# Expert weights in strips of 1024, 1024 and 768 columns over four PSUM banks, hidden rows turned in three groups and the next expert's rows in one

## What is computed

```python
def swiglu(h, w_gu, w_down):
    g, u = jnp.split(h @ w_gu, 2, axis=-1)
    return (jax.nn.silu(g) * u) @ w_down

for e in range(N_EXPERTS):                      # 8 experts, each row goes to 2
    y = y + combine[:, e:e + 1] * swiglu(xf, w_gu[e], w_down[e])
```

## Time and profile before

| what | value |
|---|---|
| median of 3 runs | 1445.33 us (1444.56 to 1445.95) |
| profiled execution | 1444.12 us |
| its span, first to last instruction | 1442.3 us |
| PE busy | 1432.8 us (99%) |
| DVE busy | 1164.7 us (81%) |
| ACT busy | 964.2 us (67%) |
| mean HBM rate | 288 GB/s over the span |
| granted TensorE clock | 1.00 |

### The profile page before, as it was taken

How to read it: one execution, slowest core, us unless ns; L and a number is a source line. 1 busy time by engine, 2 the same in 40 slices (tenths; PEclk the granted TensorE clock), 3 DMA queues, 4 the chain that set the end, 5 groups by cost and what they waited for, 6 DMA issues and landing times.

```text
span 1442.3 us, 19548 instructions
## 1 busy us (share of the span) xinstructions
PE 1432.8 (99%) x6803; PEld 1182.2 (82%) x6803; DVE 1164.7 (81%) x1244; ACT 964.2 (67%) x1050; POOL 41.5 (3%) x53
## 2 busy tenths in 40 slices
PE   9999999999999999999999999999999999999998
PEld 7888778888888888878888888888888888888886
DVE  6987756655547977657998999989999999899997
ACT  6676754444345677744677777777777777777775
POOL 2000003000000000000200000000000000000200
PEclk9999999999999999999999999999999999999999
DMA  9473458965465462448899999999999999999995
GB/s 339 158 234 117 121 162 306 318 186 179 146 235 170 165 227 98 147 155 300 301 384 386 390 361 397 396 363 392 364 396 396 355 401 365 391 391 360 360 382 214
DMA packets 212571, 414.93 MB, mean 288 GB/s; under 512 B 14188, under 2 KB 55528, under 8 KB 212504
## 3 DMA queue, kind: packets, MB, share of 16 engines
q1 hardware_dynamic: 206488, 393.42, 75.9%
q0 software_dynamic: 4976, 16.97, 3.5%
q10 hardware_dynamic: 1040, 3.68, 0.6%
HBM read 398.20 MB, written 15.81 MB: 287 GB/s over the span
## 4 chain that ended last, share of the span: by engine, by line
PE 96%; ACT 2%; DVE 2%; issue 0%; POOL 0%; DVEq 0%; ACTq 0%; POOLq 0%
PE ps L538 88%; PE ps L1086 1%; PE ps L806 1%; PE ps L949 1%; PE ps L928 1%; PE ps L936 1%; ACT w_hi L503 1%; ACT qk_t L1250 0%; PE ps L915 0%; PE ps L884 0%; PE ps L850 0%; PE ps L1067 0%; PE ps L927 0%; ACT prob L1375 0%; ACT sq L1375 0%
## 5 line engine op out<-in xcount | busy, mean ns | idle before, releaser
L508 DVE TENSOR_TENSOR w_lo<-raw,w_hi 128x2048 fp32r<-128x2048 f32 (+2 forms) x240 | 511.2, 2140 | 144.1 <-ACT w_hi L503 141.1
L503 ACT ACTIVATE w_hi<-raw 128x2048 fp32r<-128x2048 f32 (+2 forms) x240 | 431.5, 1799 | 212.8 <-PE ps L538 196.3
L538 PE MATMUL ps<-w_hi,act_hi 128*128 128x512 f32 (+1 forms) x1264 | 332.7, 393 | 0.7 <-ACT act_hi L1250 0.6
L538 PE MATMUL ps<-w_hi,act_lo 128*128 128x512 f32 (+1 forms) x1264 | 328.8, 388 | 0.0
L538 PE MATMUL ps<-w_lo,act_hi 128*128 128x512 f32 (+1 forms) x1264 | 325.1, 387 | 0.0
L538 PEld LDWEIGHTS ps<-w_lo,act_hi 128*128 128x128 f32 x1264 | 235.5, 188 | 48.9 <-DVE w_lo L508 0.5
L538 PEld LDWEIGHTS ps<-w_hi,act_lo 128*128 128x128 f32 x1264 | 234.9, 188 | 47.9
L538 PEld LDWEIGHTS ps<-w_hi,act_hi 128*128 128x128 f32 x1264 | 231.1, 188 | 46.4 <-ACT act_hi L1250 1.4
L503 ACT ACTIVATE w_hi<-raw_more 128x2048 fp32r<-128x2048 f32 x96 | 170.7, 1778 | 65.6 <-PE ps L538 64.2
L508 DVE TENSOR_TENSOR w_lo<-raw_more,w_hi 128x2048 fp32r<-128x2048 f32 x96 | 201.1, 2110 | 14.2 <-ACT w_hi L503 12.9
L508 DVE TENSOR_TENSOR w_lo<-raw_low,w_hi 128x2048 fp32r<-128x2048 f32 (+1 forms) x64 | 128.9, 2022 | 12.4 <-ACT w_hi L503 11.6
(11 more groups left out here) (284 smaller groups left out, 1273.0 us busy)
## 6 DMA issues: line engine op xcount, KB each, us to landing
raw<-in_moe_w_gu SPq DMA_DIRECT2D x192, 512.0 KB, 9.8
raw_more<-in_moe_w_gu SPq DMA_DIRECT2D x96, 512.0 KB, 10.0
raw<-in_w_in SPq DMA_DIRECT2D x72, 512.0 KB, 4.7
raw_low<-in_moe_w_gu SPq DMA_DIRECT2D x64, 512.0 KB, 9.8
raw_more<-in_moe_w_down SPq DMA_DIRECT2D x64, 512.0 KB, 6.2
raw<-in_dense_w_gu SPq DMA_DIRECT2D x44, 512.0 KB, 5.0
raw_low<-in_moe_w_down SPq DMA_DIRECT2D x32, 512.0 KB, 8.1
raw<-in_moe_w_down SPq DMA_DIRECT2D x32, 512.0 KB, 5.6
```

The lines of the kernel that those rows point to most:

```text
L503: nc.scalar.activation(w_hi[:, self.split_slot(j), 0:n], self.raw(j)[:, 0:n], ACT.Copy).then_inc(self.hi, 1)
L508: nc.vector.tensor_tensor(w_lo[:, c, 0:n], self.raw(j)[:, 0:n], w_hi[:, c, 0:n].bitcast(F32), ALU.subtract).then_inc(self.lo, 1)
L538: return nc.tensor.matmul(dst, a, b, start=start and n == 0, stop=stop and n == 2)
```

## The change

- Gate and up weights come in three strips of 1024, 1024 and 768 columns. A piece is one k-tile of a strip: 1024 gate and 1024 up columns (2048), or 768 and 768 (1536). That makes 24 pieces of gate and up.
- The down weights have 12 pieces, `EDOWN_K` = 1, 1 and ten times 2. The total stays at 36.
- A strip takes four PSUM banks: strips 0 and 2 take 0 to 3, strip 1 takes 4 to 7. Turned rows go to banks 0 and 1 (strip 0) or 4 and 5.
- A strip's turn has 8, 8 and 6 transposes. It stands after the strip's fourth successor piece (`TURN_AT` and `DOWN_TURN` are 3, counted from 0). The next expert's rows are turned in one group of 8 after down piece 7.
- tanh and the two DVE operations run once a strip over 1024 or 768 columns, 3 times an expert in place of 6. `ehid` now lies in the space of `hid`.
- The rows' weights have a tile `xw` and a small DMA of their own, and the slot counts move to bank 3 with the places: `places_done` is now signalled behind two more small matmuls.

```diff
-    EG_STRIPS = [STRIP] * (FF // STRIP) + [FF % STRIP] * (FF % STRIP > 0)
+    EDOWN_K = [1, 1] + [2] * 10
+    EG_STRIPS = [2 * STRIP, 2 * STRIP, FF - 4 * STRIP]
     EGS = len(EG_STRIPS)
-    EG_CHUNKS = [(j, k0, CHUNK // (2 * w), w) for j, w in enumerate(EG_STRIPS) for k0 in range(0, KD, CHUNK // (2 * w))]
+    STRIP_K = 2 * STRIP // P
+    EG_CHUNKS = [(j, k, w) for j, w in enumerate(EG_STRIPS) for k in range(KD)]
+    EG_BANK = (0, 4, 0)
+    TURN_AT, DOWN_TURN = 3, 3
...
+        def turn_banks(j):
+
+            b = 0 if j == 0 else 4
+            return ps[:, b:b + 2, :].rearrange("p a n -> p (a n)")
...
-            nc.tensor.matmul(ps[:, 3, E:2 * E], ones_r, chosen[:, 0, :], start=False, stop=True).then_inc(places_done, 1)
-            nc.tensor.matmul(ps[:, 2, 0:E], ones_r, chosen[:, 0, :], start=True, stop=False)
-            nc.tensor.matmul(ps[:, 2, 0:E], ones_r, chosen[:, 1, :], start=False, stop=True).then_inc(places_done, 1)
+            nc.tensor.matmul(ps[:, 3, E:2 * E], ones_r, chosen[:, 0, :], start=False, stop=True)
+            nc.tensor.matmul(ps[:, 3, 2 * E:3 * E], ones_r, chosen[:, 0, :], start=True, stop=False)
+            nc.tensor.matmul(ps[:, 3, 2 * E:3 * E], ones_r, chosen[:, 1, :], start=False, stop=True).then_inc(places_done, 1)
...
-                            for k in range(n):
-                                kk = k0 + k
-                                for hh in range(1 if w == HC else 2):
...
+                            for at in range(0, 2 * w, STRIP):
+                                mm = one_pass(p, strip_bank(j)[:, at:at + STRIP], act_hi[:, k, 0:P], act_lo[:, k, 0:P],
+                                              ch[:, at:at + STRIP], cl[:, at:at + STRIP], k == 0, k == KD - 1)
                         mm.then_inc(r.used, 1)
-                        if 1 <= j < EGS - 1 and c == STRIP_END[j] - 2:
+                        if j and k == TURN_AT:
                             hidden_turn(e, j - 1)
...
-                        if d == 0:
-                            hidden_turn(e, EGS - 2)
-                        if d == 2:
+                        if d == DOWN_TURN:
                             hidden_turn(e, EGS - 1)
-                        if not last and d in (4, 6):
...
+                        if not last and d == 7:
+                            pe.wait_ge(z["eturn_free"], strip_count(e, EGS - 1))
+                            for half in range(2):
+                                gather(e + 1, half)
...
                 def body(e, last):
-                    for c, (j, k0, n, w) in enumerate(EG_CHUNKS):
+                    for c, (j, k, w) in enumerate(EG_CHUNKS):
                         split(e, c + LEAD, last)
...
-                        if c == STRIP_END[j] - 1:
...
+                        if k == KD - 1:
+                            gate, up = strip_bank(j)[:, 0:w], strip_bank(j)[:, w:2 * w]
+                            dve.wait_ge(z["sig_ready"], strip_count(e, j))
+                            stt(esig[:, 0:w], esig[:, 0:w], 1.0, gate, ALU.add, ALU.mult).then_inc(z["sig_half"], 1)
+                            dve.wait_ge(z["sig_half"], strip_count(e, j))
...
+                            stt(ehid[:, 0:w], esig[:, 0:w], 0.5, up, ALU.mult, ALU.mult).then_inc(z["gu_free"], 1)
```

More of the change, by code:

```diff
@@ L299, in decoder_trunk @@
         raw_low = sb("raw_low", [P, 2, CHUNK], F32, experts)
-        ehid = sb("ehid", [P, STRIP], F32, experts)
-        esig = sb("esig", [P, STRIP], F32, experts)
+        esig = sb("esig", [P, 2 * STRIP], F32, experts)
         experts.close()
@@ L1073, in first_gather @@
                         dst = ps[:, FIRST_BANK[pair], k * P:(k + 1) * P]
[L1074 to L1078, removed]
+                        for t in range(1 if pair < 2 and not k else 0, TT):
+                            mm = nc.tensor.matmul(dst, xres[:, t, c:c + P], pick[:, t, :], start=t == 0, stop=t == TT - 1)
                     mm.then_inc(z["first_turned"], 1)
                 def hidden_turn(e, j):
-                    pe.wait_ge(z[f"gu_free{j % 2}"], strips_read(e, j) + 1)
-                    if j >= 2 or not is_first(e):
-                        pe.wait_ge(z[f"eturn_free{j % 2}"], turns_read(e, j))
+                    pe.wait_ge(z["gu_free"], strip_count(e, j))
+                    if j == 2:
+                        pe.wait_ge(z["eturn_free"], strip_count(e, 1))
                     for k in range(EG_STRIPS[j] // P):
-                        mm = nc.tensor.transpose(ps[:, 4 + j % 2, k * P:(k + 1) * P], ehid[:, k * P:(k + 1) * P], ident)
+                        mm = nc.tensor.transpose(turn_banks(j)[:, k * P:(k + 1) * P], ehid[:, k * P:(k + 1) * P], ident)
                     mm.then_inc(z["eturn_done"], 1)
@@ L1140, in body @@
                         pe.wait_ge(z["over"], len(TAIL) * e)
-                    for c, (j, k0, n, w) in enumerate(EG_CHUNKS):
[L1142 to L1148, removed]
+                    for c, (j, k, w) in enumerate(EG_CHUNKS):
+                        if j == 0 and first and not q and k % 2 == 0:
+                            pe.wait_ge(z["first_hi"], k // 2 + 1)
+                        elif j == 0 and not (first and not q) and k % 4 == 0:
+                            pe.wait_ge(z["x_hi"], 2 * gathers(q, e) + k // 4 - 1)
+                        if j == 1 and k == 0 and not first:
+                            if q:
+                                pe.wait_ge(z["y_half0"], e)
+                                pe.wait_ge(z["y_half1"], e)
+                            else:
+                                pe.wait_ge(z["y_copied"], e)
+                        elif j == 2 and k == 0:
+                            pe.wait_ge(z["eturn_free"], strip_count(e, 0))
@@ L1149, in body @@
                         ch, cl = r.take(pe, e, c)
-                        b = 2 * (j % 2)
                         for p in range(3):
[L1152 to L1155, removed]
+                            if p == 1 and j == 0 and first and not q and k % 2 == 0:
+                                pe.wait_ge(z["first_lo"], k // 2 + 1)
+                            elif p == 1 and j == 0 and not (first and not q) and k % 4 == 0:
+                                pe.wait_ge(z["x_lo"], 2 * gathers(q, e) + k // 4 - 1)
@@ L1219, in moe_pass @@
                 if q:
-                    pe.wait_ge(z["xs_landed"], 16)
+                    for half in range(2):
+                        gather(0, half)
                 else:
@@ L1226, in moe_pass @@
                     pe.wait_ge(pick_ready, 2)
-                for pair in range(4):
-                    first_gather(pair)
+                    for pair in range(4):
+                        first_gather(pair)
+                    pe.wait_ge(places_read, 1)
                 body(0, False)
@@ L1575, in body @@
                         act.dma_start(y_rows[e], y_sb[:]).then_inc(z["y_stored"], 16)
-                for pair in range(4):
-                    first_part(pair)
+                if q:
+                    for half in range(2):
+                        gather_part(0, half)
+                else:
+                    for pair in range(4):
+                        first_part(pair)
                 body(0, False)
@@ L2071, in body @@
                         scattered(e + 1)
-                if not q:
+                if q:
+                    for half in range(2):
+                        gather_part(0, half)
+                else:
                     moe_ring.split_lo(dve, 0, LEAD - 1)
-                first_part()
-                if not q:
+                    first_part()
                     row_lists()
```

206 lines of the change are left out of this document (85 added, 121 removed).

## The result

The changed kernel takes **1455.47 us** (median of 4 runs, 1455.34 to 1456.25) against 1444.94 us for the kernel before in the same comparison (1444.27 to 1445.95). The ratio is 1.0074, 95% interval 1.0059 to 1.0089: slower by 10.5 us. The profiled execution took 1455.37 us with a span of 1453.6 us.

The account below looks back on a forecast made before the run. PE was taken as busy throughout, with the margin of DVE's splits deciding. Terms of 10.5 + 1.0 - 1.0 + 0 gave +10.5 us on 1444.12, or 1455.8 us as median; range 1450 to 1460, chance 0.80.

Parts of the forecast that it names:

- The view: Experts: PE has no wait to take away, so the question is the splits' margin, which no busy share shows.
- Term 1: Behind the last strip: PE waits 1.31 us for down piece 3's split in every expert, 10.5 us for eight.
- Term 2: End of strip 1: PE waits 0.13 us for the split of piece 19, 1.0 us for eight experts.
- Term 3: Fewer groups of transposes: saves 0.12 us an expert, 1.0 us in all, upper bound 0.3 an expert.
- Term 4: Start: places signalled 0.22 us later, DVE loses a 0.2 us copy; taken as 0, upper bound 0.2.
- The sum: Whole kernel: +10.5 us on the profiled 1444.12; with 1.2 for the median, 1455.8 us, 0.7% slower.
- No late split: Rival, chance 0.10: DVE's total decides, not its order; no wait at down piece 3, 1443.0 to 1444.3 us.
- Loads: Rival, chance 0.03: longer packets speed PE up by removing ACT's waits for loads, 1437 to 1445 us.
- Burst at strip 0: Rival, chance 0.05: DVE later at ends of strips 0 and 1, two waits up to 0.5 us, 1457 to 1464.
- The clock: Rival, chance 0.02: PE's waits of 1.3 us let the granted clock fall to 1.2 GHz, 1478 us.

Follow-up runs that it names:

- Experiment 1: Changed kernel with down pieces of 2, 2, 1, 2, 1 and seven times 2 k-tiles: 1444.54 us, ratio 0.9999 to the kernel before.
- experiment 3: Changed kernel with the last strip's two DVE operations over 256 of its 768 columns: 1447.07 us (one run).
- experiment 6: Experiment 1's kernel with the eight transposes of the next expert's rows as four and four, behind down pieces 7 and 8: 1444.51 us.
- Experiment 8: First expert with experiment 1's strips and down pieces, the others with experiment 7's, slot counts back in bank 2: 1442.97 us, ratio 0.9987 to the kernel before.
- experiment 5: Experiment 1's kernel with gate and up weights loaded in 2 KB packets in place of 4 KB: 1444.28 us, ratio 0.9997 to the kernel before.
- experiment 7: Experiment 1's kernel with strips of 768, 1024, 1024 columns and down pieces 2, 2, 2, 1, 2, 2, 2, 1, 2, 2, 2, 2: 1445.53 us, ratio 1.0006.
- experiment 4: Kernel before the change with its experts' down pieces as 1, 1, 2, 2, 2, 1, 1, 2, 1, 1, 2, 2, 2, 2 k-tiles: 1446.15 us (one run).
- experiment 9: Experiment 8's kernel with the next expert's rows turned into banks 0 and 1 right behind the last strip's turn: 1443.65 us, ratio 0.9991.

## Why the prediction was right

The forecast was 1455.8 us, measured were 1455.47. By its own steps:

- **The view.** PE without idle time and the margin of the splits as the question: right. The busy share of PE is 99% in both kernels and says nothing of the 10 us.
- **Term 1, place and mechanism: right.** The split's start was put at T+6.21 and PE's going on at T+8.56; measured T+6.22 and T+8.56. Experiments 1 and 3 show that it takes both parts: without the two short pieces in front the wait is gone, without the wide pair 0.14 us of it are left.
- **Term 1, size: a little too small.** The wait was put at 1.31 us. Measured are 1.21 of wait, 0.08 at down piece 2 (which I had let "just pass") and 0.14 of restart, 1.43 in all. The step left out is the restart: a pass whose weight load had to wait takes longer. It could have been read ahead. In the kernel before, the pass at 697.13, from which I took the 0.06 us of the hand-over, takes 1.03 us in place of 0.91, since the next one starts here:

```profile
698.16 1.07 PE L538 MATMUL ps<-w_hi,act_hi 128*128 128x512 f32 x4
```

- **Term 2: right place, too small.** 0.13 us forecast; 0.11 of wait and 0.12 of restart measured.
- **Term 3: too small by half.** Four groups fewer were put at 0.12 us an expert, with 0.3 as bound. From the period: 93.453 - 89.76 (396 matmuls of 0.2267) leaves 3.69 us for turns before, and 94.837 - 89.76 - 1.66 leaves 3.42 after, so 0.27, and experiment 6 gives 4 x 0.072 = 0.29. Experiment 8, which has no such wait in the experts of the period, is 0.32 under the kernel before. A group's price is spread over the three or four passes behind it, and I had read only the first. In the kernel before, the passes behind a turn of four take 0.55, 0.47, 0.45 and 0.93 us from start to start, where 0.45, 0.45, 0.45 and 0.91 are usual.
- **Term 4: right in sum.** The matmuls that pick the first rows start 0.31 us later than before (683.57, before 683.26); 0.22 of it are the two small matmuls of the earlier trace rows, and 0.09 is there ahead of them. But at the split that PE waits for at 697.13 the kernel before loses 0.31 us (0.19 of wait and 0.12 of restart), and the changed kernel 0.07. Behind that pass the difference is 0.10 us (698.26, before 698.16):

```profile
697.28 1.14 PE L551 MATMUL ps<-w_lo,act_hi 128*128 128x512 f32 x4
698.26 1.07 PE L551 MATMUL ps<-w_hi,act_hi 128*128 128x512 f32 x4
```

- **The sum.** The size errors have opposite signs: +0.22 on the waits (1.66 for 1.44) and -0.15 on the groups. PE's rows give 0.1 us at the start, 1.51 to the second expert, 6 x 1.384, and 1.57 in the last: 11.5 us to the last matmuls, and 11.3 between the two profiled spans. The medians differ by 10.5, as forecast. That the forecast is within 0.4 us is luck in part: the errors cancel by two thirds, and the terms fall 0.8 us short of the profiled spans.
- **The rivals.** No late split: excluded by the eight waits. DVE's total did fall, by 8 us, where the rival's 1.4 us an expert would give 11, and PE did not gain from it. The rule that wide operations save fixed parts ("VectorE: DVE Perf Modes" of the Trainium skill, the section on the TRN2 errata) holds here, with 0.95 us on 768 columns and 0.42 on 256, and is about a sum that bounds nothing. Loads: experiment 5 shows no effect. Burst at strip 0: no wait there; the 25 waits of weight loads all lie elsewhere. The clock: 1.00 in every stretch, with PE at work over 98% of each expert and idle times of 1.2 us, so the rule of the Trainium skill's "TensorE: Matmul & The Clock Gate", Part 1, that the gate closes again with idleness, was not put to the test.

## What to carry to other kernels

Where engines hand pieces to each other a few slots ahead, cost a change by the time from the free slot to the latest moment of use, piece by piece, and not by busy shares. Wide operations saved fixed cost here but put DVE in arrears at one point; let the bound engine have long pieces while they run, and not two short ones. Measure such effects by the period of a repeated stage, which shows differences of 0.1 us here, where single runs of one kernel differ by 2 to 3.

## What the runs showed of the hardware

- A TensorE pass that had to wait for its operand took 0.12 to 0.14 us longer than one that had not, whatever the length of the wait (0.11 us or 1.21 us in the changed kernel, 1.93 in experiment 7). Where the pass started on time and only its weight load was late, it took 0.07 to 0.09 longer. That the exposed weight load is the reason is read from the PEld rows; no run varies it by itself.
- A group of transposes between matmuls costs 0.07 us beyond its transposes, and almost as much where two groups on different inputs stand back to back (0.02 saved of 0.07).
- Hand-overs were the same to 0.02 us at this place in the kernel before, the changed kernel and those of experiments 3 and 4: 0.20 from PE's next piece to ACT's copy, and 1.95 from the copy's start to DVE's split of 2048 columns. From the split's end to PE it was 0.05 to 0.06 wherever PE waited.
- Packets of 4 KB in place of 2 KB landed 0.6 us sooner in the largest group of loads and changed no time.
- In experiments 8 and 9, at periods of 93.1 us, ACT waits 2.9 and 3.1 us for a load in the last expert, and PE behind it 1.0 and 1.2. The DMA engines' share does not announce this: it is 1.00 from 1000 to 1340 us in experiment 8, where PE does not wait, and 1.01 to 1.03 there in the kernel before. That the loads are the next bound is read from these traces and was not tested.
